# First feed-forward block of a two-network kernel: the down product by seven half-size products behind all gates, modulation panels summed three per pair of chunks beside the gates

## The reference, cut to what matters

```python
c_act = jax.nn.silu(c)
for l in range(2):
    shift1, scale1, gate1, shift2, scale2, gate2 = jnp.split(c_act @ ada_w[l] + ada_b[l], 6, axis=-1)
    if l == 1:
        k_shift, k_scale = jnp.split(c_act @ kv_ada_w + kv_ada_b, 2, axis=-1)
    ...
    h = modulate(rms_norm(x, norm2_g[l]), shift2, scale2)
    x = x + gate2[:, None, :] * ((silu(h @ w_gate) * (h @ w_up)) @ w_down)
```

## Time and profile before

| | |
|---|---|
| median of 3 runs | 1122.95 us (1122.59 to 1123.61) |
| the profiled execution's own time | 1123.41 us |
| its span (first to last instruction) | 1121.6 us |
| PE busy | 1059.0 us, 94% of the span |
| DVE busy | 577.9 us, 52% |
| ACT busy | 295.6 us, 26% |
| chain that ended last | PE 82%, DVE 12%, ACT 3% |
| mean granted TensorE clock | 0.987 |

### The profile page before, as it was taken

One profiled execution on the slowest core, in us unless ns is written; L12 is line 12 of the kernel. 1 busy time (PEld: TensorE's weight loads), 2 busy tenths in 40 slices (PEclk: granted clock), 3 DMA queues, 4 the chain that ended last, 5 costly groups with the idle time before them and its releaser, 6 DMA issues.

```text
span 1121.6 us, 21217 instructions
## 1 busy us (share of the span) xinstructions
PE 1059.0 (94%) x9229; PEld 910.9 (81%) x9229; DVE 577.9 (52%) x1112; ACT 295.6 (26%) x709; POOL 64.0 (6%) x84
## 2 busy tenths in 40 slices
PE   6878999999999999889999999999997899999997
PEld 4647888888888867678999999988886688887786
DVE  8986455344421727727766575335823551602632
ACT  6512410000000645623010000133322341202641
POOL 3010010110100100000000000000003000000000
PEclk9899999999999999999999999999998999999999
DMA  9995879999945334073544552443440003644220
GB/s 290 363 310 176 300 257 370 346 329 358 329 184 189 108 116 152 31 226 122 178 152 154 181 186 84 142 151 113 131 151 4 4 4 117 203 157 124 76 76 37
DMA packets 128742, 195.78 MB, mean 175 GB/s; under 512 B 4176, under 2 KB 114394, under 8 KB 122250
## 3 DMA queue, kind: packets, MB, share of 16 engines
q1 hardware_dynamic: 118218, 131.15, 36.7%
q0 software_dynamic: 10144, 62.92, 14.8%
q10 hardware_dynamic: 288, 0.36, 0.1%
HBM read 191.53 MB, written 1.05 MB: 172 GB/s over the span
## 4 chain that ended last, share of the span: by engine, by line
PE 82%; DVE 12%; ACT 3%; issue 2%; DMA 0%; SPq 0%; DVEq 0%; ACTq 0%
PE psum L743 48%; PE psum L1129 11%; PE psum L1215 7%; PE psum L1183 6%; DVE arena L1942 4%; PE psum L1018 2%; PE psum L1721 1%; ACT arena L2978 1%; DVE sq L1942 1%; DVE arena L1948 1%; DVE arena L2112 1%; PE psum L1696 1%; DVE arena L2206 1%; ACT sq L2978 1%; DVE arena L1945 1%
## 5 line engine op out<-in xcount | busy, mean ns | idle before, releaser
L2978 ACT ACTIVATE arena<-psum 128x512 f32<-128x512 f32 (+6 forms) x229 | 102.6, 475 | 574.6 <-PE psum L743 379.3
L743 PE MATMUL psum<-hT,ring 128*128 128x256 f32 x1072 | 239.4, 380 | 2.2 <-DVE hT L1948 1.3
L743 PEld LDWEIGHTS psum<-hT,ring 128*128 128x128 f32 x1072 | 201.3, 190 | 32.8 <-issue 6.5
L743 PE MATMUL psum<-arena 64*64 64x64 f32 (+6 forms) x2252 | 91.8, 252 | 16.4 <-issue 11.6
L1942 DVE TENSOR_TENSOR arena<-arena 128x512 f32<-128x512 f32 (+8 forms) x141 | 94.9, 696 | 11.3 <-PE psum L1183 8.6
L743 PE MATMUL psum<-hT,arena 128*128 128x256 f32 (+2 forms) x664 | 95.4, 323 | 4.9 <-DVE hT L1942 4.8
L743 PEld LDWEIGHTS psum<-hT,arena 128*128 128x128 f32 (+2 forms) x664 | 83.4, 180 | 16.5 <-issue 6.7
L743 PEld LDWEIGHTS psum<-arena 64*64 64x64 f32 (+3 forms) x2252 | 72.2, 150 | 30.3 <-issue 26.4
L743 PE MATMUL psum<-ring,arena 128*128 128x256 f32 (+2 forms) x288 | 73.3, 415 | 0.5 <-ACT arena L2978 0.5
L743 PEld LDWEIGHTS psum<-ring,arena 128*128 128x128 f32 x288 | 54.5, 190 | 18.1 <-issue 7.7
L1942 DVE TENSOR_TENSOR arena<-arena,psum 128x512 f32<-128x512 f32 (+2 forms) x56 | 30.7, 569 | 73.4 <-ACT arena L2978 41.1
(11 more groups left out here) (312 smaller groups left out, 1469.3 us busy)
## 6 DMA issues: line engine op xcount, KB each, us to landing
aring<-in_ada_w POOLq DMA_DIRECT2D x36, 1024.0 KB, 8.4
ring<-in_a_w_in SPq DMA_DIRECT2D x14, 1024.0 KB, 5.4
arena<-in_ffn_w_gate SPq DMA_DIRECT2D x12, 1024.0 KB, 5.4
arena<-in_ffn_w_up SPq DMA_DIRECT2D x12, 1024.0 KB, 8.3
ring<-in_ffn_w_down SPq DMA_DIRECT2D x11, 1024.0 KB, 6.8
ring<-in_ffn_w_gate SPq DMA_DIRECT2D x10, 1024.0 KB, 8.8
ring<-in_ffn_w_up SPq DMA_DIRECT2D x10, 1024.0 KB, 9.2
ring<-in_ada_w POOLq DMA_DIRECT2D x8, 1024.0 KB, 14.5
```

The costliest lines, as they stand in the source:

```text
L743: return eng.matmul(dst, w, x, start=first, stop=last)
L2978: return eng.activation(dst, x, f, **k)
```

## The change

In layer 0 the block runs through the code of layer 1 too. `FAST` names the pairs whose gate and up products go by the seven products: none in layer 0, pairs 1 to 10 in layer 1 as before. So in layer 0

- the gate and up products stay as they are (`whole_chunks`), but all eleven pairs run back to back;
- the down product follows behind them all, in the form of layer 1: 12 panels of weights in another cut, 308 program matmuls of 128 columns in place of 176 of 256, `combine_down` and `combine_hidden` on VectorE;
- VectorE takes three modulation panels per pair: one behind the multiply of the even chunk and two behind that of the odd one; 33 panels lie ahead of the down product (three of them in pair 0), the last three in `beside_down`;
- the rows of blocks 3, 4, 5 follow pairs 2, 4, 7 on TensorE and the columns pairs 3, 5, 8; the biases stand on VectorE behind all the work of pairs 4, 6, 9. Block 6 moves into the down product;
- the token sums of pairs 0 to 7 are made in pairs 2, 4, 6, 8, those of pairs 8 to 10 behind the first two `combine_down`. In layer 1 the sums of pairs 8 and 9 also move there, and the two bank pools change places.

```diff
-        HALVED = (1,)
+        HALVED = (0, 1)
+        FAST = {0: (), 1: tuple(range(1, NDN))}
...
+            def whole_chunks(l, j, g, u):
+
+                for m in range(2):
+                    c = 2 * j + m
+                    eng.wait_ge(*next_bank(("gu", l, c)))
+                    ps = bank_of(("gu", l, c)).rearrange("p (m t) -> p m t", t=T)
+                    for i, w in enumerate((g, u)):
+                        for k in range(KC):
+                            last = mm(ps[:, i, :], w[:, k, m * P:(m + 1) * P], hT3[:, k, :], k == 0, k == KC - 1)
+                    last.then_inc(*fills(("gu", l, c)))
...
+                    if j not in FAST[l]:
+                        whole_chunks(l, j, g, u)
+                        beside(j)
+                        continue
...
                     for q in range(DOWN_PANELS):
+                        beside_down(i, q)
...
-            def swiglu(l, h_base, extra):
...
+            ROWS_AT, COLUMNS_AT = {2: 3, 4: 4, 7: 5}, {3: 3, 5: 4, 8: 5}
+
             def ada_beside(j):
 
-                if j in (2, 4, 6, 8):
-                    ada_rows(2 + j // 2)
-                if j in (3, 5, 7, 9):
-                    row_columns(2 + j // 2, row_late, "a")
-
-            swiglu(0, 0, ada_beside)
+                if j in ROWS_AT:
+                    ada_rows(ROWS_AT[j])
+                if j in COLUMNS_AT:
+                    row_columns(COLUMNS_AT[j], row_late, "a")
+
+            def ada_beside_down(i, q):
+
+                if (i, q) == (0, 2):
+                    ada_rows(6)
+                if (i, q) == (1, 1):
+                    row_columns(6, row_late, "a")
+
+            swiglu_of_halves(0, 0, ada_beside, ada_beside_down)
```

On VectorE:

```diff
                 def between(c):
+                    beside(0, c + 1)
...
+                    if j not in fast:
+                        for m in range(2):
+                            c = 2 * j + m
+                            combine_to(j + 1, m + 1)
+                            eng.wait_ge(*filled_at(("gu", l, c)))
+                            eng.wait_ge(done("silu_ready"), silus(l, c))
+                            tt(hid[:, c, :], hid[:, c, :], bank_of(("gu", l, c))[:, T:2 * T], ALU.mult)\
+                                .then_inc(*v.empties(("gu", l, c)))
+                            hid_done[0] = v.last
+                            beside(j, 1)
+                        combine_to(j + 1, 3)
+                        beside(j, 1)
+                        if j % 2 == 0 and j < NDN - 1:
+                            combine_hidden(l, [j - 2, j - 1])
+                        beside(j, 0)
+                        if j == NDN - 1:
+                            combine_down(l, 0)
+                            combine_down(l, 1)
+                        continue
...
+                combine_hidden(l, [8, 9, 10])
...
-            def ada_beside(c):
-                for _ in range(2 if c < 14 else 1):
+            def ada_beside(j, n):
+                for _ in range(n):
                     ada_panel()
-                if c in (7, 11, 15, 19):
-                    ada_bias({7: 3, 11: 4, 15: 5, 19: 6}[c])
-            swiglu(0, ada_beside)
+                if n == 0 and j in (4, 6, 9):
+                    ada_bias({4: 3, 6: 4, 9: 5}[j])
```

More of the change, by code:

```diff
@@ L2273, in combine_weights @@
                 g, u = slot(at), slot(at + 1)
-                s1, s2, s4 = [unit_sums(j)[:, x] for x in range(3)]
+                s1, s2, s4 = [unit_sums(l, j)[:, x] for x in range(3)]
                 if part == 1:
@@ L2340, in first_chunks, with swiglu_of_halves, combine_to @@
                 eng.wait_ge(*filled_at(("gu", l, 1)))
-                eng.wait_ge(done("silu_ready"), silu_base(l) + 2)
+                eng.wait_ge(done("silu_ready"), silus(l, 1))
                 tt(hid[:, 1, :], hid[:, 1, :], bank_of(("gu", l, 1))[:, T:2 * T], ALU.mult)\
                     .then_inc(*v.empties(("gu", l, 1)))
-            def swiglu_of_halves(l, h_base, behind):
+            def swiglu_of_halves(l, h_base, behind, beside=lambda j, n: None, beside_down=lambda i: None):
+                fast = FAST[l]
+                parts = [(j, part) for j in fast for part in range(1, 5)]
+                sent = [0]
+                def combine_to(j, part):
+                    while sent[0] < len(parts) and parts[sent[0]] <= (j, part):
+                        combine_weights(l, *parts[sent[0]])
+                        sent[0] += 1
@@ L2372, in swiglu_of_halves @@
                     two_ready = v.last
-                    if j < NDN - 1:
-                        combine_weights(l, j + 1, 3)
-                    else:
+                    if ahead:
+                        combine_to(j + 1, 3)
+                    if j == NDN - 1:
                         combine_down(l, 0)
@@ L2382, in swiglu_of_halves @@
                     tt(up[:, :, half_1], ps(p5), u3, ALU.add).then_inc(*v.signals("halves_read"))
-                    if j < NDN - 1:
-                        combine_weights(l, j + 1, 4)
-                    else:
+                    if ahead:
+                        combine_to(j + 1, 4)
+                    if j == NDN - 1:
                         combine_down(l, 1)
-                    if j % 2 == 0:
+                    beside(j, 1)
+                    if j % 2 == 0 and j < NDN - 1:
                         combine_hidden(l, [j - 2, j - 1])
@@ L3193, in swiglu_of_halves @@
                 for j in range(1, NDN):
+                    if j not in FAST[l]:
+                        for c in (2 * j, 2 * j + 1):
+                            eng.wait_ge(*filled_at(("gu", l, c)))
+                            act(hid[:, c, :], bank_of(("gu", l, c))[:, 0:T], ACT.Silu).then_inc(*s.signals("silu_ready"))
+                        beside(j)
+                        continue
                     nth, two = nth_of(l, j), slice(2 * j, 2 * j + 2)
```

178 lines of the change are left out of this document (74 added, 104 removed).

## The result

The changed kernel takes 1145.9 us by the median of four runs (1142.9 to 1151.9), the kernel before on the same chip 1123.3 us (1122.6 to 1125.6). The ratio is 1.0207, with a 95% interval of 1.017 to 1.0244: slower by 22.6 us, where 1151 had been forecast. The profiled execution is the longest of the four, 1151.89 us, 28.5 us over the profiled execution of before (1123.41).

The account below looks back on a forecast made before the run. TensorE's unbroken run of matmuls was taken to bound the block. Product -8.0, waits +14, +4.5, +4.5 and +8.5, block end +0.8 and clock +3.4 gave +27.7 us on 1123.4: 1151 us, range 1132 to 1163.

Parts of the forecast that it names:

- The product: Layer 0's down product: 76.8 us of pieces replaced by layer 1's form at 68.8 us, a gain of 8.0 us.
- c10: Gate chunk whose bank block 3's columns hold until VectorE's bias: TensorE waits 14 us, between 5.7 and 17.6.
- c15 and c21: Gate chunks whose banks the columns of blocks 4 and 5 hold until VectorE's bias: waits of 4.5 us each.
- The head: Start of the down product: TensorE waits 8.5 us, at least 6.8, for weight sums behind VectorE's last panels.
- The end of the block: After the last matmul, three sums and two updates follow as in layer 1: 0.8 us more.
- The clock: TensorE's granted clock falls behind the two long waits: 3.4 us lost, upper bound 6.8, lower bound none.
- The layer 1 edits: Layer 1's swap of pools and moved token sums: costed at nothing, at worst a few tenths of a us.
- Transfers are quick: Rival: only VectorE's order counts in the block, waits 5.7, 0, 0 and 6.8 us, 1129 to 1131 us; chance 0.17.
- Delays that feed on each other: Rival: upper ends everywhere, as a stalled TensorE delays VectorE's chunks; +40 us, 1163 us; chance 0.15.
- The banks are free in time: Rival: TensorE never waits in the gates or at the down product's head; 1116 us; chance 0.05.
- No bank wait, but the head's: Rival: only the wait at the down product's head occurs; -0.4 us, no measurable change; chance 0.03.

Follow-up runs that it names:

- e1: The changed kernel with the columns of blocks 3, 4 and 5 in bank pool "b" instead of "a"; 1.0157 of the kernel before.
- e9: e8 with the columns back in pool "a" and the last bias behind pair 9; 1.0046 of the kernel before.
- e2: The changed kernel with the first two down panels' weight sums ahead of the last modulation panels on VectorE; 1.0124 of the kernel before.
- e10: e8 with the first two down panels' weight sums back behind the last modulation panels; 1.0008 of the kernel before.
- e4: The changed kernel without the last 34 modulation transfers, VectorE using panels already in the slots (layer 1's modulation wrong); 1.0115 of the kernel before.
- e7: The changed kernel with 28 instead of 33 modulation panels beside the gates, pool and order of sums unchanged; 1.0127 of the kernel before.
- e8: e3 with a third panel only in pairs 1, 2, 3, 5, 7, 9 and three, two, two in the down product; 0.995 of the kernel before.
- e5: The changed kernel with 28 extra program matmuls into an unused bank in front of c10, keeping TensorE busy; 1.0274 of the kernel before.
- e3: The changed kernel with both the columns in pool "b" and the weight sums ahead of the last panels; 1.0028 of the kernel before.

## Why the prediction came out

**The mechanism was right at each place.** The three waits for a bias and the one at the head were forecast by chunk and releaser; e1 and e9 show the first by the pool alone, e2 and e10 the second by the order alone, e4 and e7 the share of the transfers. By its steps, of the profiled execution:

- *The product, -8.0.* Right within 0.5 us: without the 1.6 us of slow clock at its head the stretch takes 69.8 us, in the change and in e8, for the 69.3 that layer 1 gives. That makes -7.5.
- *c10, +14.* Measured 14.64, between the bounds 5.7 and 17.6. The bias ran at 218.96, forecast 218.8 to 221.8, and TensorE stood ready at 204.6, forecast 204.2. e4 measured the lower bound as 6.35.
- *c15 and c21, +4.5 each.* Measured 1.54 and 3.58, 3.9 us less together. The first is outside its range of 3 to 6 and inside the wider one that reached down to 0: the transfer had been asked for about when c13 ended, as forecast, and landed sooner: issued at 248.80, used at 254.87, at most 6.1 us for the 7.8 taken. The DMA share in these 6.1 us was 0.79, against 0.92 to 1.03 before, and the wait is gone altogether in e4; both speak for an emptier DMA as the reason. These two are the most mis-sized terms of the sum. The wait at c21 is inside its range of 3.4 to 6.1.
- *The head, +8.5.* Measured 7.36, between the lower bound of 6.8 and the value taken; the transfers of panels 32 and 33 had landed, so order alone was left. The same 7.4 to 7.5 appears in e4, e5 and e7.
- *The end of the block, +0.8.* From the last matmul to the first with the memory 8.0 us (393.20 to 401.19) against 6.2 before (367.16 to 373.33), 1.8 more. The further 1.0 us goes with a wait of 0.8 us for ScalarE that before has not and with a granted clock of 0.61 at 397 to 401. It belongs to this form of the product, not to the gaps: e8 has 8.1 us there.
- *The clock, +3.4.* Behind c10 1.8 us, behind the gap of c21 1.7 (8.86 for 7.17), at the head 1.6: 5.1 us. The count was short by one, since the gap of 3.6 us brought a fall too. The single fall was well priced in this execution and not in general: e4 lost 3.1 and 2.5 us. Part of that is luck, since in the first stretch of the earlier trace rows TensorE worked only 1.42 of the 2.00 us that were priced as lost clock. The upper bound of 6.8 held. The Trainium skill, "TensorE: Matmul & The Clock Gate", section "Why this matters for your kernels", has idle gaps bring the half rate back, and these rows agree for the gaps of 3.6 us and more; none is to be seen behind the 1.54 us of c15.

The layer 1 edits, costed at nothing, show nothing clear: 0.6 us more behind the block, inside the 744.9 to 750.5 of the other runs.

The waits sum to 27.1 us instead of 31.5, the clock to 5.1 instead of 3.4 and the end of the block to 1.8 instead of 0.8, so that the errors took each other off, which is luck: -7.5 + 27.1 + 5.1 + 1.8 = 26.5, against 27.7 measured for the block. The 1.2 us between are small gaps that no row here names; 0.8 more lie ahead of and behind the block.

**Against the median the forecast is 5 us high**. That it is within 1 us of the profiled execution is luck too, since this is the longest of the four; the other three are 3.4 to 9.0 us shorter. No profile shows which wait was shorter in them. That the waits for transfers move is seen in e2 (11.90 for the 14.64 of the change).

**The rivals.** *Transfers are quick* fell: VectorE waited for them ahead of c10, and the change took 1146 and not 1130; the waits it computed are those of e4. The Trainium skill, "DMA: Bandwidth & Descriptors", section "Anatomy of one DMA", by which a transfer of 1 MB would take an estimated 4.4 us, does not describe this stretch: the modulation loads of the block had a median of 7.6 us in the profile after (140 to 400 us). *Delays that feed on each other* fell too: c15's wait was shorter than expected behind the longest one, and all waits together were under the sum. *The banks are free in time* is what e8 comes near to, by its own edits. *No bank wait, but the head's* fell with the waits at c10, c15 and c21.

**What the prediction had not seen** is how the causes hide each other. The change is slower by 2.07%; mending the pool alone gives back 0.5 points, the order alone 0.8, the number of panels alone 0.8, pool and order together 1.8, and all three, with the panels placed as in e8, 2.6. Of the 20.6 us of wait in e1 the 13.3 above the change's were already there and had been covered by the waits at c10 to c21.

**Open**: why e5 lost 6 us behind the block, where the 2.6 us of e8's gain lie that its block does not show, and why the change's four runs spread over 9 us. That waits for transfers vary is one reason that fits, since e3 spreads over 11 us where the kernel before, on the same chip, spreads over 4.6 in 23 runs; but on the chip of e8 the kernel before spreads over 11 us too (1118.3 to 1129.5) and e8 over 4, so it can't be all. It wasn't tried.

## What to carry to other kernels

When a bank, a slot or a row is freed by a small instruction, ask what is written ahead of it in the same engine's stream: here 0.16 us of bias behind two panels, late in coming, and four token sums stopped TensorE for 14.6 us, some 6 of them by the order alone. Work taken out from between two stretches was also their slack; before it is taken out, list what fell due in that time and which rotation and order relied on it, since the causes cover each other and mending one only moves the wait to the next. Background work has to be dealt out by when each piece is wanted, not evenly: 28 panels beside the gates, the third one in even pairs, gave 1.0023, and 29, the third one in the pairs that needed it, 0.995. (e8 also takes one panel less beside the down product and has block 5's rows and columns one pair earlier, so that placing is not tried quite by itself.)

## What the runs showed of the hardware

- A fall of TensorE's clock did not cost in proportion to the gap ahead of it: 1.8 us behind 14.64 us of idle time (two chunks in 15.79 instead of 13.98), 3.1 us behind 6.35 (17.05), 1.7 behind 3.58, 2.3 behind 3.26 (16.27, and 0.9 more for the rows ahead). Two gaps of the same 7.36 us, at the head of the down product, cost 1.6 us in the change and 2.5 in e4; the one of 20.62 us in e1 cost 1.9 (13.69 for 11.81). Behind gaps of 1.54 (7.17) and 1.41 us there was none to be seen.
- 12.35 us of matmuls on constants in the place of the gap kept the granted clock at 1.00, but the 1.7 us gained came back as a longer next wait (4.30 us for 1.54), since there the thing waited for was the bound.
- Unchanged code can take a different time from one execution to the next by its clock: the stretch of 3509 matmuls behind layer 1 took 247.6 us in e5 at a granted clock of 0.97, 242.3 in the change at 0.99 and 238.1 in e8 at 1.00.
